# A mixture-of-experts stage: three split products on the whole array become plain fp32 products in column groups

## The chip, the cores and the metric

The kernel runs on one core of one Trainium2 chip. The metric is the device time in microseconds (us) of one execution. 2864.35 us is the median of three runs before the change (2863.68 to 2866.51).

## The reference, cut to what matters

One layer of a hybrid backbone works on 512 latent tokens and 128 prompt tokens of width 2048. The change lies in its last stage, the expert-choice mixture of experts, which latent and prompt tokens go through separately but with the same weights:

```python
def expert_choice_ffn(h, w_router, w_gate, w_up, w_down):
    cap = CAPACITY_FACTOR * n // N_EXPERTS       # 64 latent rows, 16 prompt rows
    aff = jax.nn.softmax((xf @ w_router).astype(jnp.float32), axis=-1)
    gate, idx = lax.top_k(aff.T, cap)
    xs = xf[idx]
    hid = jax.nn.silu(jnp.einsum('ecd,edf->ecf', xs, w_gate)) * jnp.einsum('ecd,edf->ecf', xs, w_up)
    ye = jnp.einsum('ecf,efd->ecd', hid, w_down) * gate[..., None].astype(xf.dtype)
    y = jnp.zeros_like(xf).at[idx.reshape(-1)].add(ye.reshape(-1, shp[-1]))
```

There are 16 experts. Each has 64 latent rows and 16 prompt rows (80 together), gate and up weights of 2048 x 1024, and down weights of 1024 x 2048, all fp32: 24 MiB (25.17 MB) an expert. The result is scaled by a modulation row (gt2), added to the tokens, and normed.

## The kernel before, in words

The program is written engine by engine, with semaphores. Up to about 1715 us of the profile it computes the mixers and the output projection. Then come the router and the top-k, on VectorE, during which TensorE has nothing to do; a gather of the first expert's 80 rows by GpSimd (L855); and the 16 experts, 15 in hardware loops and the last written out. The tail norms the output rows and stores them.

**Weights.** SyncE issues one 1 MiB load for each of the 24 pieces of an expert (`expert`, L665 to L671): eight of gate, eight of up, eight of down, into eight slots (two in `ring`, five in `hT`, one in `ar`). A load waits until the piece eight places before has been split. Seven pieces are loaded ahead of the first gather.

**Splits.** A product of precision near fp32 is made of three fast ones in the format fp32r. ScalarE copies a piece to its high part (`split_expert`, L1916), VectorE subtracts that from the piece to get the low part (`low_expert`, L2446), and TensorE then multiplies high by high, high by low and low by high (`gate_up`, L1508; `down`, L1533). The rows are split in the same way (L1902 and L2427, L1908 and L2438). There are four places for split pieces.

**One expert on TensorE.** The stationary operand is always 128 x 80 (all 80 rows together), the moving one 128 x 512. Gate and up take 16 pieces x 2 k-tiles x 3 products x 2 banks = 192 matmuls into banks 0 to 3, down takes 8 x 3 x 4 = 96 into banks 4 to 7. Between them lie the transposes of the hidden rows (`hid_transposes`, L1492, 8 of them) and of the next expert's rows (`xs_transposes`, L1484, 16).

**The other work of an expert.** ScalarE computes the silu of the gate half (L1940), VectorE the product with the up half (`hid_product`, L2433), and after the down product one instruction that multiplies by the gate of each row and by gt2 (L2551). GpSimd adds the 80 rows to their places in DRAM by an indirect DMA (L876) and gathers the rows of the expert after next (L855). VectorE norms gathered rows (`norm_xs`, L2454) once the indirect add has read its source.

**Last expert and tail.** During the last expert the 640 output rows are read back, squared on ScalarE (`y_square`, L1933), scaled on VectorE (`y_scale`, L2475) and stored. These stand among the splits of the last expert's pieces. The last expert's own rows go through L2508 (gate and gt2), L2503 (the sum with what is in DRAM), L1970, L2516, L2525 and two indirect stores.

**Plain fp32 that is there already.** Elsewhere the kernel multiplies plain fp32. Each fp32 matmul shows as two records on TensorE. L965 and L982 put four matmuls with 32 stationary columns each side by side, at partitions 0, 32, 64 and 96 of one bank (moving 128 x 512); L1308 puts two with 64 columns side by side (moving 128 x 256):

```python
for g in range(4):
    mm = pe.matmul(ps[32 * g:32 * g + 32, 6 if shift else 7, :], cond32[:, 4 * j + g, :],
                   v[:, g * BANK:(g + 1) * BANK], start=(j == 0), stop=(j == 3))
```

Of the kernel before, what the change touches and what calls it, by code (L numbers as in the profile page):

```python
# [15 lines left out]
F32 = mybir.dt.float32  # L16
# [3 lines left out]
ALU = mybir.AluOpType  # L20
ACT = mybir.ActivationFunctionType
AX = mybir.AxisListType
ds = bass.ds
# [78 lines left out]
ESLOTS = 8  # L102
# [89 lines left out]
def build(nc, T):  # L192
# [21 lines left out]
    with ExitStack() as ctx:  # L214
# [21 lines left out]
        gateT = sb("gateT", [P, NE])  # L236
# [22 lines left out]
        def hT_area(at, n):  # L259
# [79 lines left out]
        ye = area(XW + 4864, D)  # L339
        spE = split_area("split_experts", XW + 6912, SP, 2, SLOT)  # L340

        exp_slot = [ring[:, 0, :], ring[:, 1, :]] + [hT_area(i * SLOT, SLOT) for i in range(5)] + [area(XW + 6912 + SP * 2 * SLOT, SLOT)]
# [3 lines left out]
        last_rows, last_prompt = area(XW, D), area(XW + 6912, D)  # L346
# [5 lines left out]
        exp_ready = [sem(f"expert_slot_ready{s}") for s in range(ESLOTS)]  # L352
        piece_high, piece_ready, piece_used = sem("pieces_high"), sem("pieces_ready"), sem("pieces_used")
        xs_first, up_half = sem("xs_first_transposed"), sem("up_half_product_then_last_banks")
        mT_st, mT_free, mT_ld, xs_h, xs_l, hd_h = (sem("merged_stored"), sem("merged_free"), sem("merged_loaded"),
                                                   sem("xs_high"), sem("xs_low"), sem("hidden_high_then_last_rows_squared"))
# [154 lines left out]
        xs_parts = parts((0, 0, 0, 6), (6, 1, 0, 6), (12, 2, 0, 4))  # L511
        first_xs_parts = parts((0, 4, 0, 6), (6, 5, 0, 6), (12, 6, 0, 4))
        hid_parts = parts((0, 2, 0, 4), (4, 3, 0, 4))
# [91 lines left out]
        def _(sync):  # L605
# [56 lines left out]
            def expert(e, j):  # L662

                sync.wait_ge(piece_ready, e * EXP_G + (P_EXP + j + 1 - ESLOTS))
                sync.sem_inc(loads_issued, 1)  # L665
                at, out = ds(e, 1), exp_slot[j % ESLOTS]
                if j < 16:
                    src = (w_eg, w_eu)[j // 8][at, j % 8, :, :, :].squeeze(0)
                    sync.dma_start(k2(out), src).then_inc(exp_ready[j % ESLOTS], 16)
                else:  # L670
                    sync.dma_start(out, w_ed[at, :, j - 16, :].squeeze(0)).then_inc(exp_ready[j % ESLOTS], 16)  # L671

# [7 lines left out]
            for j in range(5, 7):  # L680
                expert(0, j)
            sync.wait_ge(xs_ld, 16)
            with sync.Fori(0, NE - 1) as e:
                for j in range(7, EXP_G):
                    expert(e, j)
                for j in range(7):
                    expert(e + 1, j)
            for j in range(7, EXP_G):
                expert(NE - 1, j)
# [7 lines left out]
        def _(pool):  # L697
# [209 lines left out]
            for t in range(2, NT):  # L907
                pool.wait_ge(piece_ready, (NE - 1) * EXP_G + (P_EXP + 16 + t - 2 + 1))
                load_y(t)
# [13 lines left out]
        def _(pe):  # L923
# [556 lines left out]
            def xs_transposes(lo, hi, done, bank=0):  # L1480

                for k in range(lo, hi):
                    col = k % 2 * (D // 2) + k // 2 * P
                    mm = pe.transpose(ps[:, bank + k // 6, (k % 6) * CAP:(k % 6 + 1) * CAP], ye[0:CAP, col:col + P],  # L1484
                                      ident[0:CAP, 0:CAP])
                mm.then_inc(done, 1)

            def hid_transposes(half):

                for k in range(4):  # L1490
                    col = (4 * half + k) * P
                    mm = pe.transpose(ps[:, 2 + half, k * CAP:(k + 1) * CAP], hid[0:CAP, col:col + P], ident[0:CAP, 0:CAP])  # L1492
                mm.then_inc(hd_tr, 1)

            pe.wait_ge(af_cp, 1)
            for i, (lo, hi, done) in enumerate(((0, 6, tk_tr), (6, 12, xs_first), (12, KT, xs_tr))):
                pe.wait_ge(n2_h, i + 1)
                xs_transposes(lo, hi, done, 4)
            def expert_pe(e, last):
                def gate_up(j, n, kks):  # L1500

                    bank, k0, s = 2 * (j // 8), 2 * (j % 8), j % SP
                    for kk in kks:
                        k = k0 + kk
                        for x, w in ((0, 0), (0, 1), (1, 0)):
                            for i in n:
                                col = kk * FF + i * BANK
                                mm = pe.matmul(ps[0:CAP, bank + i, :], xsT[:, x, k, :], spE[:, s, w, col:col + BANK],  # L1508
                                               start=(k == 0 and x == w), stop=(k == KT - 1 and x == 1))
                    return mm  # L1510

                pe.wait_ge(xs_l, e + 1)
                for j in range(16):
                    pe.wait_ge(piece_ready, e * EXP_G + (P_EXP + j + 1))
                    if j < 15:
                        gate_up(j, (0, 1), (0, 1)).then_inc(piece_used, 1)
                    else:
                        gate_up(j, (0,), (0, 1)).then_inc(up_half, 1)
                        gate_up(j, (1,), (0, 1)).then_inc(piece_used, 1)
                pe.wait_ge(hd_r, 2 * e + 1)  # L1520
                hid_transposes(0)
                pe.wait_ge(hd_s, e + 1)
                if not last:
                    pe.wait_ge(n2_h, e + 4)
                    xs_transposes(0, 12, xs_first)
                pe.wait_ge(hd_r, 2 * e + 2)
                hid_transposes(1)
                pe.wait_ge(ye_r, e + 1)
                if last:
                    pe.wait_ge(y_sq, 2)  # L1530

                def down(k, n, x, w):
                    return pe.matmul(ps[0:CAP, 4 + n, :], hidT[:, x, k, :], spE[:, (16 + k) % SP, w, n * BANK:(n + 1) * BANK],  # L1533
                                     start=(k == 0 and x == w), stop=(k == FT - 1 and x == 1))

                for k in range(FT):
                    pe.wait_ge(piece_ready, e * EXP_G + (P_EXP + 16 + k + 1))
                    if k % 4 == 0:
                        pe.wait_ge(hd_cp, 2 * e + (k // 4 + 1))
                    if last and k == FT - 1:  # L1540
                        for n in range(4):
                            for x, w in ((0, 0), (0, 1), (1, 0)):
                                mm = down(k, n, x, w)
                            mm.then_inc(up_half, 1)
                    else:
                        for x, w in ((0, 0), (0, 1), (1, 0)):
                            for n in range(4):
                                mm = down(k, n, x, w)
                        mm.then_inc(piece_used, 1)
                    if k == 0 and not last:  # L1550
                        xs_transposes(12, KT, xs_tr)

            with pe.Fori(0, NE - 1) as e:
                expert_pe(e, False)
            expert_pe(NE - 1, True)


        @block.scalar
        def _(act):
# [340 lines left out]
            def copy_xs(lo, hi):  # L1900
                for dst, src in xs_parts[lo:hi]:
# [677 lines left out]
```

## Time and profile before

| what | value |
|---|---|
| median of three runs | 2864.35 us |
| the profiled execution | 2866.47 us |
| its span on the core | 2864.5 us |
| TensorE busy | 2765.9 us (97%) |
| VectorE busy | 2266.7 us (79%) |
| ScalarE busy | 1608.8 us (56%) |
| mean rate of all DMA | 238 GB/s |
| mean granted clock of TensorE | 0.988 of full speed |

The profiled execution took 2866.47 us, 2.1 us over the median; its span, from the first to the last instruction, is 2864.5 us, so about 2 us lie around it. The page is of this one execution. "PE" is TensorE's matmuls, "PEld" its weight loads, which overlap them. A record of PE lasts longer than the distance to the next one, since matmuls are pipelined: rates are read from starts.

### The profile page before, as it was taken

How to read it: one execution, taken by the hardware profiler on the slowest of the kernel's cores; microseconds unless marked ns; L12 is line 12 of the kernel's file. 1: busy time of each engine (PE TensorE's matmuls, PEld its weight loads, DVE VectorE, ACT ScalarE, POOL GpSimd, SP SyncE). 2: the span in 40 equal slices, each digit the busy share in tenths (PEclk: the TensorE clock that was granted, in tenths of full speed). 3: DMA queues.
4: the chain of work that ended last, by engine and by line, in shares of the span. 5: the costliest groups of instructions: out<-in, count | busy, mean ns of one | idle time of the engine just before them, and what ended most of it. 6: DMA issues, size and time to landing. Idle time of an engine off the chain costs nothing.

```text
span 2864.5 us, 38245 instructions
## 1 busy us (share of the span) xinstructions
PE 2765.9 (97%) x13735; PEld 2058.3 (72%) x13735; DVE 2266.7 (79%) x2741; ACT 1608.8 (56%) x1976; POOL 347.3 (12%) x206
## 2 busy tenths in 40 slices
PE   7999899999899999999999997999999999999996
PEld 5788668898678888888888874666666666666664
DVE  4446777788878878888765558999989999998987
ACT  4345434445744443433444445777777777777775
POOL 0000000000000000000013000222222222222231
PEclk9999999999999999999999998999999999999998
DMA  9832113443034444544474447999999999999997
GB/s 356 304 105 78 52 54 118 138 140 100 1 111 154 144 164 152 167 154 152 165 282 126 143 155 290 402 401 385 389 378 390 389 397 378 398 386 385 385 371 292
DMA packets 175065, 682.84 MB, mean 238 GB/s; under 512 B 14548, under 2 KB 14756, under 8 KB 119164
## 3 DMA queue, kind: packets, MB, share of 16 engines
q1 hardware_dynamic: 159504, 613.45, 56.7%
q0 software_dynamic: 13392, 67.79, 7.8%
q8 instruction: 58, 0.95, 0.1%
q10 hardware_dynamic: 2064, 0.26, 0.1%
q14 instruction: 47, 0.39, 0.0%
HBM read 649.88 MB, written 31.65 MB: 238 GB/s over the span
## 4 chain that ended last, share of the span: by engine, by line
PE 87%; DMA 5%; DVE 5%; issue 2%; ACT 1%; SPq 0%; DVEq 0%; POOLq 0%; POOL 0%; ACTq 0%
PE ps L1019 40%; PE ps L1508 19%; PE ps L1533 12%; PE ps L1038 5%; DMA y_rows<-ar,sidx 4%; PE ps L1045 3%; DMA ring<-w_mod 1%; PE ps L965 1%; DVE split_experts L2446 1%; PE ps L1297 1%; PE ps L1149 1%; PE ps L1184 1%; PE ps L1308 1%; DVE ar L2264 1%; PE ps L1484 1%
## 5 line engine op out<-in xcount | busy, mean ns | idle before, releaser
L1019 PE MATMUL ps<-split_weights,split_tokens 128*128 128x512 f32 x5040 | 1159.9, 391 | 3.7 <-DVE split_tokens L547 3.3
L1019 PEld LDWEIGHTS ps<-split_weights,split_tokens 128*128 128x128 f32 x5040 | 943.0, 188 | 210.7 <-issue 9.7
L1508 PE MATMUL ps<-split_experts,split_xsT 128*80 128x512 f32 x3072 | 710.6, 392 | 2.7 <-DVE split_experts L2446 2.6
L1508 PEld LDWEIGHTS ps<-split_experts,split_xsT 128*80 128x80 f32 x3072 | 454.5, 148 | 256.1 <-DVE split_experts L2446 5.6
L540 ACT ACTIVATE split_weights<-ring 128x512 fp32r<-128x512 f32 x368 | 233.1, 633 | 672.4 <-PE ps L1019 595.0
L2446 DVE TENSOR_TENSOR split_experts<-hT,split_experts 128x2048 fp32r<-128x2048 f32 x240 | 538.6, 2284 | 16.5 <-ACT split_experts L1916 16.5
L1916 ACT ACTIVATE split_experts<-hT 128x2048 fp32r<-128x2048 f32 x240 | 461.5, 1927 | 122.1 <-PE ps L1508 86.6
L544 DVE TENSOR_TENSOR split_weights<-ring,split_weights 128x512 fp32r<-128x512 f32 x368 | 254.3, 691 | 324.2 <-ACT split_tokens L541 320.0
L1533 PE MATMUL ps<-split_experts,split_hidT 128*80 128x512 f32 x1536 | 361.0, 394 | 2.0 <-DVE split_experts L2446 1.2
L1533 PEld LDWEIGHTS ps<-split_experts,split_hidT 128*80 128x80 f32 x1536 | 225.2, 148 | 126.3 <-issue 4.0
L2446 DVE TENSOR_TENSOR split_experts<-ring,split_experts 128x2048 fp32r<-128x2048 f32 x96 | 219.9, 2291 | 36.5 <-ACT split_experts L1916 34.9
L547 DVE TENSOR_TENSOR split_tokens<-hT,split_tokens 128x640 fp32r<-128x640 f32 x288 | 237.4, 824 | 0.0
L1916 ACT ACTIVATE split_experts<-ring 128x2048 fp32r<-128x2048 f32 x96 | 185.1, 1929 | 82.4 <-PE ps L1508 51.3
L427 DVE SCALAR_TENSOR_TENSOR cst<-ring,cond,cst 128x512 f32<-128x512 f32 x300 | 213.3, 747 | 0.0
L541 ACT ACTIVATE split_tokens<-hT 128x640 fp32r<-128x640 f32 x288 | 208.7, 725 | 0.0
L1038 PE MATMUL ps<-split_tokens,split_weights 128*128 128x384 f32 x768 | 180.1, 343 | 0.0
L876 POOL DMA_INDIRECT y_rows<-ar,sidx x15 | 136.4, 9093 | 265.6 <-DVE ar L2551 231.9
L1045 PE MATMUL ps<-split_tokens,split_weights 128*128 128x256 f32 x768 | 133.6, 283 | 3.0 <-ACT ar L1751 1.8
L1038 PEld LDWEIGHTS ps<-split_tokens,split_weights 128*128 128x128 f32 x768 | 125.1, 189 | 14.3 <-issue 10.9
L1045 PEld LDWEIGHTS ps<-split_tokens,split_weights 128*128 128x128 f32 x768 | 123.2, 188 | 4.0 <-ACT ar L1751 2.1
L2446 DVE TENSOR_TENSOR split_experts<-ar,split_experts 128x2048 fp32r<-128x2048 f32 x48 | 109.9, 2290 | 13.4 <-ACT split_experts L1916 13.4
L1916 ACT ACTIVATE split_experts<-ar 128x2048 fp32r<-128x2048 f32 x48 | 92.2, 1921 | 34.1 <-PE ps L1508 21.6
(346 smaller groups left out, 2098.5 us busy)
## 6 DMA issues: line engine op xcount, KB each, us to landing
ring<-w_mod SPq DMA_DIRECT2D x96, 1024.0 KB, 5.7
hT<-w_exp_gate SPq DMA_DIRECT2D x80, 1024.0 KB, 8.7
hT<-w_exp_up SPq DMA_DIRECT2D x80, 1024.0 KB, 8.6
hT<-w_exp_down SPq DMA_DIRECT2D x80, 1024.0 KB, 7.5
ring<-w_in SPq DMA_DIRECT2D x60, 1024.0 KB, 5.1
ring<-w_exp_gate SPq DMA_DIRECT2D x32, 1024.0 KB, 8.2
ring<-w_exp_up SPq DMA_DIRECT2D x32, 1024.0 KB, 9.0
ring<-w_exp_down SPq DMA_DIRECT2D x32, 1024.0 KB, 10.6
```

The lines of the kernel that those rows point to most:

```text
L427: dve.scalar_tensor_tensor(acc, v, c, acc, ALU.mult, ALU.add).then_inc(z_rd, 1)
L540: self.eng.activation(spW[:, s, 0, :], raw, ACT.Copy)
L541: self.eng.activation(spX[:, s, 0, :], (src[k] if type(src) is dict else src[:, k, :]), ACT.Copy).then_inc(piece_high, 1)
L544: a = self.eng.tensor_tensor(spW[:, s, 1, :], raw, spW[:, s, 0, :].bitcast(F32), ALU.subtract)
L547: self.eng.tensor_tensor(spX[:, s, 1, :], (src[k] if type(src) is dict else src[:, k, :]), spX[:, s, 0, :].bitcast(F32), ALU.subtract).the ...
L1019: mm = pe.matmul(ps[:, b, :], spX[:, s, x, b * P:(b + 1) * P], spW[:, s, w, :], start=(k == 0 and x == w), stop=(k == n_k - 1 and x == 1))
L1038: mm = pe.matmul(ps[:, c, 0:TA], spW[:, s, w, c * P:(c + 1) * P], spX[:, s, x, 0:TA], start=(k == 0 and x == w), stop=(k == KT - 1 and w = ...
L1045: mm = pe.matmul(ps[:, 4 + c // 2, (c % 2) * TB:(c % 2 + 1) * TB], spW[:, s, w, c * P:(c + 1) * P], spX[:, s, x, TA:TOK], start=(k == 0 an ...
L1508: mm = pe.matmul(ps[0:CAP, bank + i, :], xsT[:, x, k, :], spE[:, s, w, col:col + BANK], start=(k == 0 and x == w), stop=(k == KT - 1 and x ...
L1533: return pe.matmul(ps[0:CAP, 4 + n, :], hidT[:, x, k, :], spE[:, (16 + k) % SP, w, n * BANK:(n + 1) * BANK], start=(k == 0 and x == w), st ...
L1916: act.activation(spE[:, s, 0, :], exp_slot[j % ESLOTS], ACT.Copy).then_inc(piece_high, 1)
L2446: dve.tensor_tensor(spE[:, s, 1, :], exp_slot[j % ESLOTS], spE[:, s, 0, :].bitcast(F32), ALU.subtract)\
```

## The change

- The splits of the expert stage go: no high and low parts, no copies of weights.
- All expert products are plain fp32. The 64 latent rows are the stationary operand twice, at array columns 0 to 63 and 64 to 127, and each of the two multiplies another 512 columns of the weights (`half_rows`). The 16 prompt rows are the stationary operand four times, in groups of 32 columns, each with another 512 columns (`quarter_rows`).
- Gate and up pieces come in turn, and one pair of pieces (two k-tiles) is multiplied as latent gate, latent up, prompt gate and up. In the down product the prompt's part of a piece follows two pieces behind the latent's.
- The hidden rows are now 128 x 512 (latent) and 48 used partitions x 512 (prompt); there are 4 transposes of 128 x 128 and 4 of 48 x 128.
- The gate of each row is applied with the product of silu and up (`hid_products`), and what is left after the down product is gt2 (`prompt_rows`, `sample_rows`, six instructions in place of one).
- There are 16 slots for pieces, of which 12 are loaded ahead of the first gather. The loops of SyncE and TensorE hold two experts.
- In the last expert, the squares and scales of the output rows stand after the hidden rows.

The diff, cut to its core:

```diff
-ESLOTS = 8
+ESLOTS = 16
-        xsT = split_area("split_xsT", XW, 2, KT, CAP)
-        hidT = split_area("split_hidT", XW + 2560, 2, FT, CAP)
-        hid = area(XW + 3840, FF)
-        spE = split_area("split_experts", XW + 6912, SP, 2, SLOT)
+        xsT = area(XW, KT, CAP)
+        hidT = area(XW + 1280, 4, 2 * CAP_L)
+        hidT_c = area(XW + 1792, 4, 48)
+        hid, hid_c = area(XW + 1984, BANK), area(XW + 1984 + BANK, BANK)
...
+        half_rows = [slice(h * CAP_L, (h + 1) * CAP_L) for h in range(2)]
+        quarter_rows = [slice(32 * g, 32 * g + CAP_C) for g in range(4)]
...
+                def sample_pair(p, kind):
+                    w = exp_piece(b, 2 * p + kind)
+                    for k in (2 * p, 2 * p + 1):
+                        for h, rows in enumerate(half_rows):
+                            col = k % 2 * FF + h * BANK
+                            mm = pe.matmul(ps[rows, kind, :], xsT[:, k, 0:CAP_L], w[:, col:col + BANK],
+                                           start=(k == 0), stop=(k == KT - 1), skip_group_check=True)
+                    return mm
+                def prompt_pair(p):
+                    for k in (2 * p, 2 * p + 1):
+                        for g, rows in enumerate(quarter_rows):
+                            col = k % 2 * FF + g % 2 * BANK
+                            mm = pe.matmul(ps[rows, 2, :], xsT[:, k, CAP_L:CAP], exp_piece(b, 2 * p + g // 2)[:, col:col + BANK],
+                                           start=(k == 0), stop=(k == KT - 1), skip_group_check=True)
+                    return mm
+                for p in range(8):
+                    if p % 3 == 0:
+                        pe.wait_ge(xs_cp, e * 3 + (p // 3 + 1))
+                    loaded(2 * p)
+                    if p < 7:
+                        sample_pair(p, 0)
+                        sample_pair(p, 1)
+                        prompt_pair(p).then_inc(exp_used, 2)
+                    else:
+                        sample_pair(p, 0).then_inc(up_half, 1)
+                        prompt_pair(p).then_inc(up_half, 1)
+                        sample_pair(p, 1).then_inc(exp_used, 2)
                 if not last:
                     pe.wait_ge(n2_h, e + 4)
+                    pe.wait_ge(hd_s, e * 2 + 1)
+                    xs_transposes(0, 6, xs_first)
+                pe.wait_ge(hd_r, e * 3 + 2)
+                hid_transposes(0)
+                if not last:
+                    xs_transposes(6, 12, xs_first)
+                pe.wait_ge(hd_r, e * 3 + 3)
+                hid_transposes(1)
+                prompt_hid_transposes()
                 pe.wait_ge(ye_r, e + 1)
...
+                for i in range(2, FT - 2 if last else FT):
+                    if i % 2 == 0:
+                        loaded(16 + i)
+                    sample_down(i, 0)
+                    sample_down(i, 1)
+                    if i == 2:
+                        pe.wait_ge(hd_cp, e * 3 + 3)
+                    prompt_down(i - 2).then_inc(exp_used, 1)
...
+            def hid_products(e, col):
+                dve.wait_ge(hd_s, e * 2 + 2)
+                v = hid_c[64:112, :]
+                dve.scalar_tensor_tensor(v, v, gateT[64:112, 1, col], ps[64:112, 2, :], ALU.mult, ALU.mult).then_inc(hd_r, 1)
+                dve.wait_ge(exp_used, e * EXP_G + 16)
+                for half in range(2):
+                    v = hid[:, half * 2 * P:(half + 1) * 2 * P]
+                    dve.scalar_tensor_tensor(v, v, gateT[:, 0, col], ps[:, 1, half * 2 * P:(half + 1) * 2 * P],
+                                             ALU.mult, ALU.mult).then_inc(hd_r, 1)
```

## Rows read from the trace of the kernel before

**Rows 1.** Stretches: us; PE, PEld, DVE, ACT, POOL busy; clock, DMA share, GB/s.
```profile
1813.16:2769.86 956.70, 953.52 (x4370) 619.62 (x4369) 868.09 (x463) 723.18 (x448) 228.36 (x54) 1.00 1.00 389
1881.20:1949.25 68.05, 68.01 (x313) 44.30 (x312) 62.00 (x34) 51.66 (x33) 15.54 (x4) 1.00 1.01 399
1904.00:1920.00 16.00, 16.00 (x72) 10.30 (x71) 16.00 (x8) 13.12 (x9) 0.00 (x0) 1.00 1.01 425
```
**Rows 2.** The timeline of TensorE over one expert (start us, us).
```profile
1881.20 44.22 PE L1508 MATMUL ps<-split_experts,split_xsT 128*80 128x512 f32 x192
...
1925.54 0.99 PE L1484 MATMUL ps<-cst,ar 80*128 80x80 f32 x12
```
**Rows 3.** Who waited for whom, experts 1 to 14 (us in total, times, longest us).
```profile
ACT split_experts L1916 <- PE ps L1508: 139.9, 183, 0.9
DVE ar L2454 <- POOLq L879: 29.2, 14, 2.7
PE ps L1508 <- DVE split_experts L2446: 2.6, 6, 0.6
```
**Rows 4.** DMA queues of experts 1 to 14 (packets, MB, share of 16 engines).
```profile
q1 hardware_dynamic: 48697, 354.62, 92.2%
q0 software_dynamic: 2592, 17.76, 8.0%
```
**Rows 5.** The timeline of TensorE where four groups of 32 columns stand between full products.
```profile
118.95 0.52 PE L1045 MATMUL ps<-split_tokens,split_weights 128*128 128x256 f32 x3
119.31 0.69 PE L1038 MATMUL ps<-split_tokens,split_weights 128*128 128x384 f32 x3
119.84 0.52 PE L1045 MATMUL ps<-split_tokens,split_weights 128*128 128x256 f32 x3
120.29 1.93 PE L965 MATMUL ps<-ring,cond 128*32 128x512 f32 x16
122.03 1.04 PE L982 MATMUL ps<-ar 128*32 128x512 f32 x8
...
123.00 0.81 PE L1038 MATMUL ps<-split_tokens,split_weights 128*128 128x384 f32 x3
```
**Rows 6.** TensorE's weight loads there, the passes of four one after the other.
```profile
121.17 0.13 PEld L965 LDWEIGHTS ps<-ring,cond 128*32 128x32 f32 x4 [0.30 <-issue]
...
122.03 0.13 PEld L982 LDWEIGHTS ps<-ar 128*32 128x32 f32 x4 [0.30 <-issue]
```
**Rows 7.** The timeline of TensorE where pairs of 64-column groups stand among transposes.
```profile
700.65 1.52 PE L1308 MATMUL ps<-ar 128*64 128x256 f32 x12
...
717.62 0.65 PE L1308 MATMUL ps<-ar 128*64 128x256 f32 x4
718.20 0.65 PE L1297 MATMUL ps<-cst,ar 128*128 128x128 f32 x4
718.79 1.51 PE L1308 MATMUL ps<-ar 128*64 128x256 f32 x12
```
**Rows 8.** Groups by line, experts: instructions near those added (busy us, mean ns).
```profile
L2433 DVE TENSOR_TENSOR ar<-ar,ps 80x512 f32<-80x512 f32 x32 | 21.8, 683 | 9.3 <-PE ps L1508 9.3
L2438 DVE TENSOR_TENSOR split_hidT<-ps,split_hidT 128x320 fp32r<-128x320 f32 x32 | 15.6, 488 | 1.4 <-ACT split_hidT L1908 0.5
```
**Rows 9.** The timeline before the first expert's products, all engines.
```profile
1742.02 0.57 ACT L1922 ACTIVATE split_xsT<-ps 128x480 fp32r<-128x480 f32 x1 [12.29 <-PE ps L1484]
...
1743.41 45.93 PE L1508 MATMUL ps<-split_experts,split_xsT 128*80 128x512 f32 x192
```
**Rows 10.** The timeline of the last expert on TensorE and of the tail on VectorE.
```profile
2769.86 44.22 PE L1508 MATMUL ps<-split_experts,split_xsT 128*80 128x512 f32 x192
2818.02 0.50 PE L1492 MATMUL ps<-cst,ar 80*128 80x80 f32 x4 [3.95 <-DVE ar L2433]
...
2841.58 3.00 PE L1533 MATMUL ps<-split_experts,split_hidT 128*80 128x512 f32 x12 [1.24 <-DVE split_experts L2446]
...
2849.05 2.36 DVE L2516 TENSOR_TENSOR ar<-ar,ring 80x1024 f32<-80x1024 f32 x2
```

More of the change, by code:

```diff
@@ L681, in _ @@
                 expert(0, j)
+            sync.wait_ge(lg_pe, 5)
+            for j in range(7, 12):
+                expert(0, j)
             sync.wait_ge(xs_ld, 16)
[L683 to L689, printed above, removed]
+            for j in range(12, ESLOTS):
+                expert(0, j)
+            with sync.Fori(0, NE // 2 - 1) as n:
+                for g in range(ESLOTS, 2 * EXP_G + ESLOTS):
+                    expert(n, g)
+            for g in range(ESLOTS, 2 * EXP_G):
+                expert(NE // 2 - 1, g)
             sync.wait_ge(kv_st, 32)
@@ L1528, in expert_pe @@
                 pe.wait_ge(ye_r, e + 1)
[L1529 to L1551, printed above, removed]
@@ new lines, in prompt_down @@
+                def prompt_down(i):
+                    k, w = down_order[i], exp_piece(b, 16 + i)
+                    for g, rows in enumerate(quarter_rows):
+                        mm = pe.matmul(ps[rows, 6, :], hidT_c[:, k % 4, k // 4 * 32:k // 4 * 32 + CAP_C], w[:, g * BANK:(g + 1) * BANK],
+                                       start=(i == 0), stop=(i == FT - 1), skip_group_check=True)
+                    return mm
+                pe.wait_ge(hd_cp, e * 3 + 1)
+                loaded(16)
@@ new lines, in expert_pe @@
+                if not last:
+                    for i in range(FT - 2, FT):
+                        prompt_down(i).then_inc(exp_used, 1)
+                    return
+                loaded(16 + FT - 2)
+                for i in range(FT - 4, FT):
+                    mm = prompt_down(i)
+                mm.then_inc(up_half, 1)
+                for c in range(2):
+                    for i in range(FT - 2, FT):
+                        mm = sample_down(i, c)
+                    mm.then_inc(up_half, 1)
@@ L1558, in _ @@
+            with pe.Fori(0, NE // 2 - 1) as n:
+                for b in range(2):
+                    expert_pe(n, b, False)
+            expert_pe(NE // 2 - 1, 0, False)
+            expert_pe(NE // 2 - 1, 1, True)
         @block.scalar
@@ L2441, in low_expert @@
[L2441 to L2447 removed]
+            ch.step(dve.memset(gateT[:, 1, :], 0.0))
+            for rows in half_rows:
+                dve.tensor_tensor(gateT[rows, 0, :], first[:, 0, :], turned[:, 0, :], ALU.max)
```

293 lines of the change are left out of this document (117 added, 176 removed).

## The prediction, made before the changed kernel was run

> **What bounds the kernel now.** I read the busy times by stretch first. In experts 1 to 14 TensorE is busy 953.52 of 956.70 us at a full granted clock, 68.34 us an expert; an undisturbed expert takes 68.05 us [rows 1]. So TensorE sets the pace there. Its timeline gives the parts: 192 gate and up matmuls in 44.22 us, 0.23 us each, 96 down matmuls at the same rate (22.1 us), and 24 transposes at some 0.07 us (0.99 us for twelve, less the tail of the last) [rows 2]. The sum is 68.0 us. Second, the waits: ScalarE, which opens the splits, waits for TensorE to give places back and never for a load. VectorE waits 29.2 us in 14 times for GpSimd, because the norm of gathered rows needs the indirect add to have read its source; the splits behind that norm come late, TensorE stands (2.6 us as matmuls, more in its weight loads), and that is how 68.05 becomes 68.34 [rows 3]. Third, the DMA queues: their packets fill 92.2% + 8.0% of the sixteen engines' time [rows 4]. The DMA is nearly full too, and what TensorE could win is limited by that.
>
> **The new cost of TensorE, by terms.** In the trace four plain fp32 matmuls of 32 columns show as eight records, that is two passes of four, and the passes follow one another at 0.43 us (121.17 to 122.03 is two) with 512 moving columns each [rows 6]. Sixteen records from 120.29 to 122.03 are four passes in 1.74 us, 0.43 each and 0.02 once [rows 5]. So four groups really run side by side. For pairs of 64 columns, with 256 moving columns, twelve records take 1.52 us, of which 0.38 is the length of the last (also 0.65 less one pass and the first weights): six passes at 0.22 [rows 7]. With 512 moving columns I take 0.43 too: either form then moves 1.2 columns a nanosecond in each group.
> - *Passes.* Gate and up: 16 k-tiles x 2 matrices x one pair, and 16 x one group of four for the prompt, 48 sets. Down: 8 x 2 pairs and 8 groups of four, 24 sets. 72 sets x 2 passes x 0.43 = 61.9 us. Before, the matmuls took 66.3.
> - *Changes of form.* Three full-array records of 256 columns take 0.36 us up to the next full-array one (118.95 to 119.31), but 0.45 up to the first of the 32-column form (119.84 to 120.29): 0.09 to enter. Leaving: 122.03 + 2 x 0.43 = 122.89, and the next starts at 123.00: 0.11 [rows 5]. A pair of 64 columns between transposes takes 0.58 (717.62 to 718.20) where its two passes are 0.43, and the four transposes behind it 0.59 (to 718.79) where they are 0.44: 0.15 for each change, first weights with it [rows 7]. A direct change between 64 and 32 columns has no row. Between bounds of nothing and 0.23 us (the dearest one shown: 0.11 to leave 32 columns, and 0.12 by which the 0.81 of the three records behind it exceeds the usual 0.69 [rows 5]) I take what the same ends cost against the full array, 0.12 into 32 columns (0.10 + 0.02) and 0.16 back into 64 (0.11 + 0.05), as the nearest rows. The new order has 14 changes into the prompt's form (8 in gate and up, 6 in down) and 14 back (8, 5, and one into the next expert): 14 x 0.28 = 3.9 us. Five more with the full array or the 48-row transposes at 0.15 make 0.8. In all 4.7 us.
> - *Transposes.* 16 of rows at 0.07, 4 of 128 columns at 0.11 (a quarter of 0.44 as above), 4 small ones at up to 0.07: 1.8 us.
> - *The turn from up to down.* The first half of the product with up can start only when the last up matmul has ended, some 0.2 us after the place of the next one. A VectorE instruction of 80 x 512 takes 0.68 us and one of 128 x 320 takes 0.49 [rows 8], so 128 x 256 takes about 0.45. TensorE has six row transposes (0.4 us) and a change of form beside it, and then stands about 0.2 us. The second half is hidden by the next six; the silus and the prompt's product run beside the last up matmuls, which take 1.7 us.
>
> 61.9 + 4.7 + 1.8 + 0.2 = 68.6 us an expert. That is 0.55 more than an undisturbed expert of before and 0.26 more than the mean one. The gain of 4.4 us in passes is given back in changes of form.
>
> The rule that speaks against this change stands in the Trainium skill, "TensorEngine Tiling (Array Packing)", under Key Properties: changing the tiling mode, not merely the tile, drains TensorE. The rows agree for each change to or from the full array; none shows 64 against 32. By the rule the 28 direct changes all pay, and the period is the 68.6 above.
>
> **What else the change touches.** The splits go from ScalarE and VectorE (62.00 and 51.66 us of 68.05 [rows 1]); they are not what ends last, so that is worth only the late norm, 0.29 us an expert, counted above. Instead of one instruction after down VectorE has six, some 5 us (four of 0.68 [rows 8] and two twice as wide); the indirect add is issued up to 5 us later, and what hides it is that the next norm is needed only some 40 us on, at the end of the next gate and up. Without that cover those 5 us would stand in every expert. Sixteen slots in place of eight: at no time did a split wait for a load, so it costs and brings nothing by itself; it is cover for the DMA. The five loads that now go ahead of the first gather (5.2 MB, 12 us at 425 GB/s) share the engines with the stores of rows before the top-k; the top-k lies between them and the gather, and I put nothing for them. SyncE's waits change from splits to used pieces; nothing but loads is queued behind them.
>
> *Start.* The first product starts at 1743.41, after the low part of the rows; now it waits only for ScalarE's copy, which ends at 1742.59, and a tenth for the step: 0.7 us earlier [rows 9]. The clock is low at first: 45.93 us for the first gate and up against 44.22. I keep that 1.7.
>
> *Last expert.* It took from 2769.86 to 2844.58, 74.7 us, because squares and scales stood among the splits (3.95 us idle before L1492, 1.24 before L1533, and a lowered clock after the idle) [rows 10]. In the new one they come after the hidden rows, beside the down product. Without row transposes but with a longer turn I put 68.1.
>
> *Tail.* From the last matmul's end to the last L2516 pair's start it took 4.5 us (2844.58 to 2849.05), in which VectorE was behind [rows 10]. Now five instructions of 0.68 remain after it: 3.4. That is 1.1 less.
>
> **Sum.** Before, first gate and up to the last matmul: 1743.41 to 2844.58. After: 1742.7 + (68.6 + 1.7) + 14 x 68.6 + 68.1 = 2841.5, and 1.1 from the tail: 4.2 us less. The profiled execution, 2866.5 us, would come to 2862.3, and the median, 2.1 under it, to 2860.2. I say 2861, since a turn costs rather more than less. A difference under 0.2%, 5.7 us, cannot be told from none.
>
> **The rivals.**
> - *A, the direct changes are free, and the DMA becomes the bound.* If 64 and 32 columns can follow each other without a gap (for it: both divide the array's columns; against it: every change shown costs), TensorE needs 68.6 - 28 x 0.10 = 65.8 us. The DMA then counts. At 425 GB/s, which it reaches in a stretch with weights alone [rows 1], 25.17 MB take 59.2 us, and the other queue's 8.0% [rows 4] is 5.5 more: 64.7 at least; at most it is full already, 68.05. In the middle, 66.4: 15.5 experts x 2.2 = 34 us less, 2827 (2820 to 2852).
> - *B, a direct change costs more than one with the full array.* The mechanism is that TensorE drains and the new form's weights are loaded bare, several of them each time. At the dearest price shown, 0.23 in place of 0.14, it is 2.5 us an expert and 40 in all: 2901. It decides early: the mean change needs only 0.16 us for the kernel to be slower by 0.2%, since 28 x 16 x 0.02 is 9 us. For it: no row shows two forms of column groups in turn, and 448 such turns come. Against it: the entries into 32 columns are the cheapest, with 0.02 of bare weights.
> - *C, the pairs of 64 do not overlap with 512 moving columns.* 48 sets would take twice as long, 41 us an expert, 3520 in all. Rows 7 speak against it; 1 in 100.
>
> **How the numbers follow.** The computed case has 62 in 100, A 14, B 20, C and others (a load that comes late, a longer turn) 4. Around the computed 2861 I hold 2850 to 2872: 0.02 us in a change is 9 us, 0.003 in a pass is 7. Of it 0.24 falls under 2858.6, 0.33 within 5.7 us of 2864.35, 0.05 above. With A below and B above: faster 0.37, same 0.35, slower 0.28. The range takes in A and the lower half of B: 2822 to 2893.
>
> **What would show it.** Right: 68.6 us from one gate and up to the next; passes at 0.43; gaps of 0.12 to 0.16 around each prompt group; TensorE waiting for neither loads nor VectorE but for 0.2 us a turn; VectorE under 12 us an expert; a DMA share still near 1. A shows as gaps gone and TensorE waiting for loads. B shows as gaps of 0.2. Wrong altogether it is if passes of pairs start 0.86 apart, or if the period is 68.6 for another reason.

## The result, and the profile after

The kernel after takes **2927.99 us** (median of 4 runs, 2924.81 to 2932.17), the kernel before, on the same chip, 2864.76 us (4 runs). The ratio is 1.0214, with a 95% interval from 1.0202 to 1.0226: **slower by 2.1%**, outside the predicted range of 2822 to 2893 us. The profiled execution took 2924.81 us with a span of 2922.8.

First the stretches, beside [rows 1]: the first expert, the second, nine microseconds behind it, and the rest of one turn of TensorE's loop (us; PE, PEld, DVE, ACT, POOL busy; clock, DMA share, GB/s).

```profile
1743.28:1813.84 70.56, 70.43 (x410) 18.95 (x409) 3.98 (x4) 6.75 (x12) 4.13 (x8) 0.97 1.02 377
1813.84:1882.50 68.66, 68.45 (x412) 18.49 (x408) 9.17 (x10) 4.92 (x9) 2.85 (x4) 1.00 1.02 394
1882.50:1891.54 9.04, 1.07 (x3) 0.19 (x4) 5.19 (x6) 0.00 (x0) 1.47 (x1) 0.77 1.01 415
1891.54:2029.30 137.76, 137.53 (x814) 37.64 (x813) 13.14 (x14) 9.84 (x18) 4.06 (x7) 0.99 0.96 365
```

The first two experts are what was predicted: 70.56 us (70.3 predicted, low clock at the start), and 68.66 to the end of the second one's last matmul. Then TensorE does almost nothing for 9 us. Its timeline shows what is there (start us, us, idle time before).

```profile
1813.84 3.65 PE L1538 MATMUL ps<-ar 128*64 128x512 f32 x16
1817.42 1.91 PE L1547 MATMUL ps<-ar 128*16 128x512 f32 x16
1819.26 3.65 PE L1538 MATMUL ps<-ar 128*64 128x512 f32 x16
...
1879.64 2.77 PE L1589 MATMUL ps<-ar 128*16 128x512 f32 x24
1886.12 1.07 PE L1538 MATMUL ps<-ring,ar 128*64 128x512 f32 x2 [3.71 <-issue]
1891.54 1.98 PE L1538 MATMUL ps<-ring,ar 128*64 128x512 f32 x4 [4.35 <-issue]
```

The second expert's last products end at 1882.4, and the first products of the third start one by one, after 3.71 and 4.35 us of "issue": the engine waited for no semaphore that the profile knows. It is the place where the loop of two experts goes back to its first instruction; from here on this is called a return. Among TensorE's waits from the first expert on it is by far the largest, and no load is among them. The waits for VectorE's splits of [rows 3] are gone too: VectorE still waits for the indirect add before its norm (150.0 us in 14 times), but TensorE no longer waits for VectorE behind it (us in total, times, longest).

```profile
PE ps L1538 <- issue: 44.8, 12, 4.5
PE ps L1510 <- DVE ar L2482: 0.6, 1, 0.6
```

Twelve waits are two at each of six returns. With them one turn (two experts) takes 146.8 to 148.9 us. What the engine waits for is in the queues. In the stretch of [rows 4], 1813.16 to 2769.86, the kernel before moved packets in two queues. The kernel after has a third that counts:

```profile
q1 hardware_dynamic: 45339, 330.20, 86.7%
q0 software_dynamic: 2496, 17.11, 8.4%
q8 instruction: 57, 0.93, 0.4%
```

The 57 packets of 16.4 KB are instructions, TensorE's own, as the experiments with its loop show. They come nine to a turn: three at the return (starts at 1883.3, 1888.9 and 1895.3 us, around the two waits), the others spread over the turn. Over the whole execution the queue has 120 packets, against 58 before. So the program of the loop is fetched anew in every turn. One packet, called a page here, holds some 256 instructions: while the first two experts run for the first time, packets start 21.6 us apart in the mean (1788.9 to 1875.2), and at the 1656 instructions in 137.0 us of an undisturbed turn that is about 260.

The rest of the profile answers to rows shown before. The turn from up to down, and the end:

```profile
1857.39 0.63 PE L1503 MATMUL ps<-cst,ar 80*128 80x80 f32 x6
1857.60 0.87 DVE L2482 SCALAR_TENSOR_TENSOR ar<-ar,gateT,ps 128x256 f32<-128x256 f32 x2 [0.46 <-PE ps L1538]
1858.13 0.20 PEld L1510 LDWEIGHTS ps<-cst,ar 128*128 128x128 f32 x2 [0.27 <-DVE ar L2482]
...
2899.38 2.79 DVE L2493 TENSOR_TENSOR ar<-ps,ar 16x512 f32<-16x512 f32 x4 [1.87 <-PE ps L1589]
2902.19 1.41 DVE L2489 TENSOR_TENSOR ar<-ps,ar 64x512 f32<-64x512 f32 x2
...
2907.47 2.36 DVE L2543 TENSOR_TENSOR hT<-ar,ring 80x1024 f32<-80x1024 f32 x2
```

TensorE stands 0.1 to 0.3 us in the turn from up to down, where 0.2 was predicted; the two halves of the product overlap and take 0.87 us together. At the end VectorE finishes the prompt's four instructions only at 2902.2, when the last matmul starts, and all the rest comes behind them.

### The profile page after: what moved, and what is told of

Same layout as the page of the kernel before. It is cut to its first block, busy times and chain, and to the rows that moved or that the text cites. A ratio compares the mean times of both kernels' runs of the same rounds, so it can differ in the third digit from the quotient of the medians.

```text
span 2922.8 us, 39396 instructions
## 1 busy us (share of the span) xinstructions
PE 2787.5 (95%) x15271; PEld 1653.1 (57%) x15271; DVE 1422.4 (49%) x2375; ACT 861.7 (29%) x1609; POOL 143.2 (5%) x206
## 4 chain that ended last, share of the span: by engine, by line
PE 92%; DVE 3%; issue 2%; DMA 1%; ACT 1%; SPq 0%; POOL 0%; POOLq 0%; DVEq 0%; ACTq 0%
PE ps L1038 39%; PE ps L1538 16%; PE ps L1547 8%; PE ps L1581 8%; PE ps L1057 5%; PE ps L1589 4%; PE ps L1064 3%; DMA ring<-w_mod 1%; PE ps L984 1%; PE ps L1168 1%; PE ps L1316 1%; PE ps L1327 1%; DVE ar L2312 1%; PE ps L1203 1%; PE ps L1295 1%
## 5 line engine op out<-in xcount | busy, mean ns | idle before, releaser
L1982 ACT ACTIVATE ar<-ps 128x512 f32<-128x512 f32 x16 | 9.6, 597 | 957.9 <-PE ps L1538 957.9
L1538 PE MATMUL ps<-ar 128*64 128x512 f32 x1152 | 266.2, 599 | 0.0
L2478 DVE SCALAR_TENSOR_TENSOR ar<-ar,gateT,ps 48x512 f32<-48x512 f32 x16 | 12.1, 754 | 464.1 <-ACT ar L1984 464.1
L2493 DVE TENSOR_TENSOR ar<-ps,ar 16x512 f32<-16x512 f32 x64 | 44.0, 688 | 365.0 <-PE ps L1589 364.3
L1538 PEld LDWEIGHTS ps<-ar 128*64 128x64 f32 x1152 | 75.6, 136 | 186.9 <-issue 186.9
L1547 PE MATMUL ps<-ar 128*16 128x512 f32 x1152 | 152.6, 595 | 0.0
L1538 PE MATMUL ps<-hT,ar 128*64 128x512 f32 x640 | 147.9, 600 | 0.0
L1581 PE MATMUL ps<-ar 128*64 128x512 f32 x576 | 137.3, 603 | 0.0
L1538 PE MATMUL ps<-ring,ar 128*64 128x512 f32 x256 | 77.9, 706 | 44.8 <-issue 44.8
L2500 DVE SCALAR_TENSOR_TENSOR ar<-ar,cst 80x2048 f32<-80x2048 f32 (+2 forms) x18 | 38.0, 2118 | 168.0 <-POOLq L898 150.0
L1538 PEld LDWEIGHTS ps<-hT,ar 128*64 128x64 f32 x640 | 41.7, 136 | 104.8 <-issue 104.8
```

The costliest lines, as they stand in the source:

```text
L1538: mm = pe.matmul(ps[rows, kind, :], xsT[:, k, 0:CAP_L], w[:, col:col + BANK], start=(k == 0), stop=(k == KT - 1), skip_group_check=True)
L1547: mm = pe.matmul(ps[rows, 2, :], xsT[:, k, CAP_L:CAP], exp_piece(b, 2 * p + g // 2)[:, col:col + BANK], start=(k == 0), stop=(k == KT - 1) ...
L1581: mm = pe.matmul(ps[rows, 4 + c, :], hidT[:, k % 4, half_rows[k // 4]], w[:, col:col + BANK], start=(i == 0), stop=(i == FT - 1), skip_gro ...
```

## The experiments

The question was what a return costs, why, and whether the rest of the prediction holds without it.

**140 instructions ahead of the loop.** How the loop lies in its pages depends on how many instructions stand ahead of it. Shifting it changes nothing in the loop itself. The added instructions, called fillers, are increments of a semaphore that nobody waits for.

```diff
+            for _ in range(140):
+                pe.sem_inc(fillers, 1)
             pe.wait_ge(tk_d, 1)
```

> The changed kernel with 140 semaphore instructions put into TensorE's program ahead of the expert loop, where TensorE is idle anyway during the top-k (140 x 0.05 us = 7 us of some 10). In the changed kernel TensorE stands for about 10 us each time its loop of two experts (1656 records a turn) begins again, and packets of 16 KB of the instruction queue come in there. Theory P (pages): what counts is how many 16 KB pages of 256 instructions a turn touches; by the times of the packets it touches eight now, and 140 instructions later seven. Then the six stalls go: 2862 to 2868 us. Theory S (size): a turn of 1656 instructions is too long wherever it lies: 2928. Theory D (data): the stall comes from the loads of the first pieces of the slots: 2928.

Measured: 2871.97 us (10 runs), ratio 1.0022 (1.0012 to 1.0032). Every turn takes 137.0 us, and no instruction packet moves in the loop. From 1882 to 2700 us its queues are

```profile
q1 hardware_dynamic: 41470, 301.95, 91.0%
q0 software_dynamic: 2282, 15.64, 8.6%
```

and at the place of the return the timeline runs on. But the fillers stood in the open. The small product ahead of which they stand had waited 10.5 us for VectorE; now TensorE comes to it after 21.18 (some 0.15 us for a filler, where 0.05 was expected), and the transposes behind it start at 1751.09, in the kernel after at 1740.91.

```profile
1740.77 0.25 PE L1483 MATMUL ps<-cst,ar 48*64 48x48 f32 x1 [21.18 <-issue]
...
1751.09 2.43 PE L1506 MATMUL ps<-cst,ar 80*128 80x80 f32 x16 [8.38 <-DVE ar L2503]
```

So 56 us go in the medians in spite of 10 us of a later start. Slots, loads, products and their order are those of the kernel after, which rules them out as the cause; what is left is the loop's position or the fillers themselves, and the next run tells these apart.

**256 instructions ahead of it**, a whole page.

```diff
+            for _ in range(50):
+                pe.sem_inc(fillers, 1)
             pe.wait_ge(af_r, 1)
...
+            for _ in range(206):
+                pe.sem_inc(fillers, 1)
             pe.wait_ge(tk_d, 1)
```

> The same with 256 such instructions, a whole page: the loop lies in its pages as in the changed kernel. Theory P: the stalls are back, 2928 (up to 2 more if the fillers do not fit the idle time). Theory S and D: 2928 as well. If both this and the 140 are fast, it is not the position that matters but something that the fillers do.

Measured: 2952.73 us (4 runs), ratio 1.0301 (1.0283 to 1.0318); turns of 147.0 to 149.0 us, as without fillers. The stalls are back, and the whole execution has 121 instruction packets, one more than the kernel after. The total is larger than that of the kernel after because the fillers, again in the open, make the transposes start at 1768.65, 28 us later: the expectation had allowed only 2 us for them. A shift by a whole page brings the old state back and one by 140 does not: it is the place within a page that counts, not the presence of fillers.

**96 instructions beside other work.** The same cure, put where TensorE's queue had time: two fillers after each of the 16 k-tiles of three projections, long before the experts.

```diff
                 def with_gated_rows(k):
+                    for _ in range(2):
+                        pe.sem_inc(fillers, 1)
```

> The changed kernel with 96 semaphore instructions in TensorE's program, two after each k-tile of three projections long before the expert loop, where TensorE's sequencer is far ahead of its matmuls. They move the loop of two experts by 96 places. Theory P (eight 16 KB pages a turn are reloaded, seven are not): no stall at the returns, and nothing paid for the fillers, where the 140 ahead of the top-k cost 8.6 us: 2863 (2861 to 2866). If a plain length limit held, or if the 140 helped by their place in time, the stalls come back: 2928.

Measured: **2862.35 us** (11 runs, 2860.42 to 2863.82; before 2866.58), ratio 0.9985 (0.9976 to 0.9994). Experts 2 to 15 take 68.50 us each, start to start (68.51 in the mean). The windows view, the same columns as above, for a stretch of fourteen such periods and for 550 us of it:

```profile
1813.54:2772.55 959.01, 957.37 (x5716) 258.97 (x5712) 129.83 (x140) 67.62 (x125) 39.97 (x54) 1.00 0.99 388
2100.00:2650.00 550.00, 549.06 (x3276) 148.61 (x3274) 74.40 (x80) 39.37 (x72) 22.04 (x32) 1.00 0.99 386
```

TensorE has 549.06 of 550 us busy at a full clock. This is the kernel that the prediction had priced, with 96 fillers added. In its profiled execution the last group of matmuls starts at 2838.16 and ends at 2841.8, where 2841.5 was predicted.

```profile
2835.47 2.76 PE L1592 MATMUL ps<-ar 128*16 128x512 f32 x24
2838.16 3.65 PE L1584 MATMUL ps<-ar 128*64 128x512 f32 x16
```

**The kernel before with three experts a turn.** This asks whether the reload needs anything of the change at all.

```diff
-            with pe.Fori(0, NE - 1) as e:
-                expert_pe(e, False)
+            with pe.Fori(0, (NE - 1) // 3) as n:
+                for b in range(3):
+                    expert_pe(n * 3 + b, False)
```

> The kernel before, with TensorE's loop written as five turns of three experts (1968 instructions) in place of fifteen turns of one; nothing else. Theories P and S: it is reloaded at each of four returns, about 10 us each: 2905 (2895 to 2910). Theory D, or any that needs the plain fp32 products or sixteen slots: 2865.

Measured: 2902.91 us (4 runs), ratio 1.013 (1.0113 to 1.0147), and turns of 213.5 to 214.4 us where three experts were 205.0. That is 8.9 us a return in the mean, and the four returns make 36 of the 38 us. The old products, in a long loop, stall in the same way, and the packets are there (queue of the stretch of [rows 4]):

```profile
1945.69 3.79 PE L1533 MATMUL ps<-split_experts,split_hidT 128*80 128x512 f32 x16
1951.61 0.89 PE L1508 MATMUL ps<-split_experts,split_xsT 128*80 128x512 f32 x2 [2.13 <-DVE split_experts L2447]
1957.08 5.26 PE L1508 MATMUL ps<-split_experts,split_xsT 128*80 128x512 f32 x12 [4.58 <-issue]
```

```profile
q8 instruction: 44, 0.72, 0.3%
```

The row of 1951.61 shows how such a wait can hide: it is put down to VectorE, whose semaphore was the last one seen, but two instruction packets start around it, at 1948.8 and 1954.5 us.

**One expert a turn in the kernel after**, on TensorE and on SyncE, which needs twelve slots, since 24 pieces must fill them a whole number of times.

```diff
-ESLOTS = 16
+ESLOTS = 12
...
-            with pe.Fori(0, NE // 2 - 1) as n:
-                for b in range(2):
-                    expert_pe(n, b, False)
-            expert_pe(NE // 2 - 1, 0, False)
-            expert_pe(NE // 2 - 1, 1, True)
+            with pe.Fori(0, NE - 1) as n:
+                expert_pe(n, 0, False)
+            expert_pe(NE - 1, 0, True)
```

> The changed kernel with loops of one expert a turn on TensorE and SyncE (828 instructions), which needs a number of slots that divides 24: twelve in place of sixteen. Theories P and S: no stall; at 68.6 us an expert as inside the turns of the changed kernel, 2861 to 2866. Theory D: stalls stay, or come in every expert, since there are fewer slots: 2928 or more.

Measured: 2867.26 us (10 runs), ratio 1.0005 (0.9995 to 1.0014). Each turn takes 68.50 or 68.51 us and nothing is reloaded, though the loop begins at the old place. The total misses the expected range by a microsecond or so, and the timeline says where:

```profile
2832.74 1.05 PE L1589 MATMUL ps<-ar 128*16 128x512 f32 x8
2836.65 5.29 PE L1589 MATMUL ps<-ar 128*16 128x512 f32 x32 [2.85 <-DMA ar<-w_exp_down]
```

With twelve slots one of the last down pieces comes late, and the first four passes behind the wait run at a lower clock: 0.83 to 0.85 us apart in place of 0.43, with 0.50 granted from 2836.7 to 2840.0. So the other four slots are worth 4 to 5 us at the end, and nothing in the loop.

**The kernel after with short loads.** The same instructions and the same position, but every load behind the first sixteen is cut to 128 of its 2048 columns; most weights of the experts are left out. It asks why a return costs ten microseconds.

```diff
-                    sync.dma_start(k2(exp_slot[s]), src).then_inc(exp_ready[s // 2], 16)
+                    dst = k2(exp_slot[s])
+                    if g >= ESLOTS:
+                        dst, src = dst[:, :, 0:64], src[:, :, 0:64]
+                    sync.dma_start(dst, src).then_inc(exp_ready[s // 2], 16)
                 else:
...
+                    n_cols = 2 * FF if g < ESLOTS else 128
```

> The kernel after with every weight load behind the first sixteen cut to an eighth or a sixteenth of its width (64 columns of each half, or 128), so that the sixteen DMA engines are nearly idle during the experts; most of each expert's weights are therefore left out, the same instructions run. It asks why one return of TensorE's loop costs some 10 us. Theory L (the instruction packets stand in the DMA rings behind the weight loads, several descriptors of 1 us and more in each): with the loads gone each packet is there in under 1.5 us, the three of a return cost 2 to 4 us together, a turn takes 139 to 141 us in place of 147.4, and the total is 2875 to 2890. Rival F (a fixed cost of each fetch, whatever else moves): a turn stays at 146 to 149 us and the total at 2920 to 2930. The passes themselves stay at 0.43 in both.

Measured once: 2898.24 us, turns of 142.8 to 143.4 us. Neither theory holds as written: with 137.0 as the turn without a return, one costs 6.2 us, between L's 2 to 4 and F's 9 and more. The first return looked so, and from 2100 to 2650 us the DMA share was 0.19 and the clock 0.99:

```profile
1882.35 1.07 PE L1542 MATMUL ps<-ring,ar 128*64 128x512 f32 x2 [1.09 <-issue]
1885.32 5.29 PE L1542 MATMUL ps<-ring,ar 128*64 128x512 f32 x14 [1.91 <-issue]
```

```profile
2100.00:2650.00 550.00, 534.95 (x3132) 146.12 (x3130) 72.41 (x79) 37.15 (x70) 20.78 (x29) 0.99 0.19 41
```

So the full loads are worth about 4 of the 10.4 us of a return. The two waits of the first return are 3.0 us in all against 8.1 with full loads, and its three packets start 3.2 and 3.5 us apart against 5.6 and 6.4. That the packets stand behind the loads in the queues' order fits this, but was not shown apart from other effects of the loads. The other 6.2 us remain with the DMA engines nearly idle: two waits and four passes at a lower clock behind them. They were not taken apart further, and this kernel has one run only.

**Half the changes of form**, on the kernel with 96 fillers: the prompt's groups of two pairs of pieces stand together, 7 trips into the 32-column form and back in place of 14. Same products, same passes.

```diff
                         sample_pair(p, 0)
                         sample_pair(p, 1)
-                        prompt_pair(p).then_inc(exp_used, 2)
+                        if p % 2:
+                            prompt_pair(p - 1)
+                            prompt_pair(p).then_inc(exp_used, 4)
...
-                    if i == 2:
+                    if i == 3:
                         pe.wait_ge(hd_cp, e * 3 + 3)
-                    prompt_down(i - 2).then_inc(exp_used, 1)
+                    if i % 2:
+                        prompt_down(i - 3).then_inc(exp_used, 1)
+                        prompt_down(i - 2).then_inc(exp_used, 1)
```

> As the kernel with 96 fillers beside the projections, with the prompt's products of two pairs of pieces (gate and up) and of two pieces (down) made together: 7 round trips between the 64- and the 32-column form an expert in place of 14, the same matmuls. My theory that a round trip costs 0.27 us: 7 x 0.27 = 1.9 us off the 68.5 of an expert, 66.6, if the loads can follow: 30 us less than the kernel with fillers alone, 2833. Rival: the DMA's floor lies at 67 to 68 us an expert, and TensorE then waits for loads: 2841 to 2857.

Measured: **2833.38 us** (4 runs, 2832.72 to 2834.42), ratio 0.9885 (0.987 to 0.990): faster than the kernel before and than that with fillers alone. A turn takes 133.17 us, 66.59 an expert, so seven round trips are 1.92 us, 0.27 each.

```profile
2100.00:2650.00 550.00, 549.07 (x3368) 163.72 (x3364) 73.34 (x80) 39.98 (x73) 22.04 (x32) 1.00 1.02 399
```

TensorE still has 549.07 of 550 us busy and waits for no load, though the DMA share is now 1.02.

**The same merging with one expert a turn**, so that no filler is needed.

```diff
-ESLOTS = 16
+ESLOTS = 12
...
+                        if p % 2:
+                            prompt_pair(p - 1)
+                            prompt_pair(p).then_inc(exp_used, 4)
```

> One expert a turn with twelve slots (828 TensorE instructions a turn, which needs no filler at any place), and the prompt's groups merged two by two, 7 round trips of form in place of 14. If both findings add up: 66.6 us an expert as with the fillers, no return stalls, and the last expert as in the run with one expert a turn, 4 us longer by its late down load: 2867.3 - 16 x 1.92 = 2836.6, between 2832 and 2842. If twelve slots are too few cover for the later release of the merged groups (the DMA share is near 1), TensorE waits for loads in each expert: 67.5 or more, 2850 and up.

Measured: 2840.13 us (4 runs), ratio 0.9908 (0.9892 to 0.9925). Each turn takes 66.59 us, so both findings add up in the loop. The last expert pays more than before for the twelve slots: two waits for down pieces.

```profile
2803.18 5.29 PE L1584 MATMUL ps<-ar 128*64 128x512 f32 x16 [4.35 <-DMA ar<-w_exp_down]
...
2812.92 5.32 PE L1592 MATMUL ps<-ar 128*16 128x512 f32 x32 [2.61 <-DMA ar<-w_exp_down]
```

**Where the DMA would set the pace.** The kernel with fillers, with the prompt's products left out but for their first k-tiles (seven eighths of the prompt's share), all loads kept.

```diff
-                        sample_pair(p, 1)
-                        prompt_pair(p).then_inc(exp_used, 2)
+                        mm = sample_pair(p, 1)
+                        (prompt_pair(p) if p == 0 else mm).then_inc(exp_used, 2)
...
-                    sample_down(i, 1)
+                    mm = sample_down(i, 1)
                     if i == 2:
                         pe.wait_ge(hd_cp, e * 3 + 3)
-                    prompt_down(i - 2).then_inc(exp_used, 1)
+                        mm = prompt_down(0)
+                    mm.then_inc(exp_used, 1)
```

> As the kernel with 96 fillers beside the projections, without the prompt's products but for the first k-tiles of gate, up and down (left out: seven of eight of the prompt's share of every expert product; its rows in the output are not the reference's). TensorE needs only about 45 us an expert, so the loads set the time. Estimate from the kernel before (weights at 425 GB/s, 59.2 us, and 5.5 us for the gather and the indirect add): 65 to 66 us an expert, 2815 in all. Rival: the DMA is already full in the kernel before, 68 us an expert, 2855.

Measured: 2822.83 us (4 runs), ratio 0.9848 (0.9833 to 0.9863). Turns take 132.0 to 132.3 us, **66.1 us an expert**, at the upper end of the 65 to 66 expected; the total is 8 us over the 2815. Now TensorE waits for loads, and its clock is lower between them (waits from 1820 us on, then the window):

```profile
PE ps L1541 <- DMA ar<-w_exp_up: 90.2, 44, 4.4
PE ps L1583 <- DMA ar<-w_exp_down: 68.5, 16, 4.9
PE ps L1541 <- DMA hT<-w_exp_up: 25.8, 15, 7.9
```

```profile
2100.00:2650.00 550.00, 443.45 (x2034) 142.53 (x2036) 73.68 (x81) 43.10 (x79) 23.33 (x35) 0.92 1.01 400
```

With half the changes an expert takes 66.59 us, half a microsecond above what the loads allow. More merging could win that half microsecond in each of the 16 experts, an estimate of 8 us in all; it was not tried.

## Why the prediction was wrong

**The step that failed is one that is missing.** Under "what else the change touches" the prediction went through slots, waits, gathers and VectorE, and never asked what it costs that the loops "hold two experts", as the list of changes says. The diff changes the loop over experts on TensorE from one expert to two, and each product by column groups is made of more instructions: TensorE's records grow from 656 to 1656 a turn. At its position that is enough for TensorE to fetch its program anew in every turn. The prediction put nothing for it, and six returns cost 10.4 us each, 62 us in all. The last matmul of the kernel after starts 61.0 us later than that of the kernel with 96 fillers (2902.21 against 2841.22), although its experts begin 2.0 us earlier. The profiled spans differ by the same 61.0, the medians by 65.6: the profiled execution of the kernel after is 3.2 us under its median, that of the kernel with fillers 1.5 us over its own.

The trace of before could have raised the question, not answered it. Its loop of gates has 1610 TensorE records a turn, near to 1656, and from 1130 to 1490 us, while it runs, the queue q8, which in the kernel after carries TensorE's code, has no packet over two returns (the eight packets below are another queue's):

```profile
q1 hardware_dynamic: 26458, 52.55, 43.2%
q0 software_dynamic: 1603, 10.28, 7.6%
q14 instruction: 8, 0.07, 0.1%
```

The prediction lacked a rival "the longer loop is fetched again", with six returns as its factor; for its price before had no row.

The Trainium skill, "Runtime: NRT & Kernel Launch", section "Instruction fetch mechanics", says that TensorE's instruction memory holds 2048 instructions, refilled in blocks of 256, and that a taken branch out of "the current 2-page window" forces a fetch. The runs bear out the blocks: packets of 16.4 KB, and a shift by 256 as good as none. The window they do not: 1610 records a turn in the gate loop, and 1656 shifted by 96 or 140, stay without any packet; here the measurement decides. Counted in blocks of 256, 1656 and 1610 instructions touch seven blocks or eight, as they are placed, and the 1968 of the long loop of before at least eight. All five cases tried (0, 96, 140 and 256 fillers, and the long loop of before) and the gate loop fit a memory in which seven blocks can be kept and eight can't. That count is argued from these runs; it was not measured by itself.

**Passes: right.** Eight passes of 64-column pairs take 3.65 us and four of the prompt's groups 1.91, tail included. A step of latent gate, latent up and prompt takes 5.42 us (1813.84 to 1819.26), which is 12 passes of 0.429 and 0.27 more.

**Changes of form: right.** Predicted 0.28 a round trip from the nearest rows, against bounds of nothing and 0.46; measured 0.27, once by that step and once by taking seven away. By the starts in that step, entering the 32-column form takes 0.11 (0.12 predicted) and going back 0.16 (as predicted). Rival A (free) and rival B (0.23 each way) both fall. A's own sum has a slip: it takes 0.10 off for each of 28 changes where the terms had priced them at 0.14, so TensorE would need 64.7 us and not 65.8. A's time does not hang on it, since it goes by the DMA's 66.4. The Trainium skill, "TensorEngine Tiling (Array Packing)", Key Properties, has the rule that a change of mode drains the engine; the trace agrees in so far as every change between 64 and 32 columns costs time, 0.13 us on average.

**The period: right without the reload.** 68.6 predicted, 68.50 measured. First expert: 70.3 predicted, 70.56 measured in the kernel after and 70.2 with fillers.

**The last expert and the tail: errors that cancel.** The last expert was put at 68.1; in the run with fillers it is 67.3 (2774.56 to 2841.81). The tail was to shrink by 1.1 us, since only five instructions of 0.68 were to remain after the last matmul. It takes 4.7 us up to the last pair of sums (2841.81 to 2846.48), not 3.4. VectorE's four instructions on the prompt's rows start only when the prompt's last down product is done, take 2.79, and end when the last matmul starts (2841.2), so that nothing of the chain of eight behind them had begun. The two errors are 0.8 and 1.3 us in opposite directions; that they nearly cancel is luck.

**The sum.** 2860 to 2861 predicted for the priced kernel, 2862.35 measured with fillers (2860.5, if its ratio of 0.9985 is laid on the 2864.76 us of the first chip). The start was 2.6 us later than predicted there (1745.29 against 1742.7; 2.0 of it is the difference to the kernel after, which starts at 1743.28), and fourteen experts of 68.50 and a last one of 67.3 made 2.2 us of that good. The terms were sound but for the tail; the one not among them was fifteen times the 4.2 us that they gave.

**The DMA as the next bound: right.** Put at 64.7 to 68.05 with 66.4 as the middle; measured 66.1. TensorE never waited for a load in the loop before it came there.

## What to carry to other kernels

When a diff makes a loop body longer on an engine, count that engine's instructions a turn, and look in the queues for instruction packets inside loops; waits put down to "issue" at the same place in every turn are their mark. A loop kept short, or unrolled less, costs nothing inside the loop here and takes the risk away (the 4 to 5 us at the end are the price of twelve slots). Fillers ahead cure it too, but the next edit of the code in front can bring it back. Where forms of matmul alternate, group those of one form: taking away half the round trips was worth 1.0% here (2862.35 to 2833.38).

## What was not expected of the hardware

- A return of a loop of 1656 TensorE instructions costs 10.4 us or nothing, by where its first instruction stands: with 0 and 256 instructions ahead it costs, with 96 and 140 it doesn't. The packets fetched are only some 0.4% of the DMA engines' time.
- The cost of a return depends on the traffic: 10.4 us at a DMA share near 1, 6.2 at 0.19 (one run). In the first return of both, two waits follow one another, with one pass between them.
- After the stall the clock is granted lower. It was 1.00 in the first 3.5 us after the last products (1882.5 to 1886.0), 0.63 in the 5.5 us with the lone pass and the second wait, and 0.55 from 1891.54 to 1894.50, where the passes start 0.80 to 0.91 us apart, about twice the 0.43: the lower of the clock's two levels, 1.2 GHz. Behind that it was 1.00 and they were back at 0.43. A wait of 2.85 us for a load in the last expert (twelve slots) was followed by the same, at 0.50.
- An instruction that only increments a semaphore takes some 0.15 us on TensorE: 140 of them stand in 21.18 us and 206 in 31.15. The 96 beside other work cost at most the 2.0 us by which the transposes start later (1742.92 against 1740.91).
